# Projection products that stream their moving operand from the last column to the first

## The chip, the cores and the metric

One core of a Trainium2 chip runs the whole program. The metric is device time in microseconds (us) of one launch. The kernel before took 895.56 us in the median of three runs (894.59 to 895.74).

## The reference, cut to what matters

Two transformer-like blocks in float32 over one sequence of 256 tokens and a model width of 1024. The first block normalizes x, multiplies it by `w_in` (1024 x 8280), runs a gated delta rule over 8 heads and a sparse attention with an indexer, multiplies by `w_out`, and adds an MLP with squared ReLU (1024 x 4096 and 4096 x 1024). The second block has an input projection (1024 x 3592), retention and forgetting attention, a cross attention to 256 memory rows, and a gated MLP with hidden width 2816.

```python
proj = h @ w_in                                        # first block
x = x + merged @ w_out
x = x + jnp.square(jax.nn.relu(h2 @ w_mlp_up)) @ w_mlp_down
proj = hn @ w_in                                       # second block
h = h + (jax.nn.silu(hn @ w_gate[l]) * (hn @ w_up[l])) @ w_down[l]
```

The change touches only how the products of activations with weight matrices (the projections) are streamed through TensorE. What is computed stays the same: every output column is the same sum, in the same order over the contracted dimension.

## The kernel before, in words

**Blocks and chunks.** Every weight matrix is cut into column blocks, mostly 512 wide (`NCOL`); some are 300, 260 or 256 wide. The list `blocks` (lines 122 to 152) holds them in the order in which they are computed. A block is loaded in chunks of `CK` = 4 row tiles of 128, into a ring of four slots (`raw`, and in the same ring `w_hi` and `w_lo`). SyncE issues the loads (`load`, line 398); a load waits on `mm_done` of the chunk four before it.

**Split numbers.** A float32 operand is carried as two float32r parts. ScalarE writes `w_hi` from `raw` (line 1273), VectorE (line 1826), or in a few chunks GpSimd (line 2638), writes `w_lo` as the rest. The activations are turned by TensorE, and lie as `s_hi` and `s_lo` (or `hT_hi`, `hT_lo`, `h2_hi`, `h2_lo` for the two down projections), with 128 rows of the contracted dimension on the partitions and the 256 tokens along the free dimension. A product then takes three matmuls: high by high, high by low, low by high.

**`mm` (line 477).** It computes one block for all 256 tokens, two row tiles of the contraction at a time (a "pair", or "quarter" of a block of eight tiles). `product` (line 493) issues one matmul: the stationary operand is a 128 x 128 piece of the activations, the moving operand is a row tile of the weight chunk, `width` columns wide, and the output is bank `G[b % 2][t]`, for token tile t. All the matmuls of a block accumulate in the same two banks; consecutive ones mostly alternate between the banks. Two sets of two banks alternate between blocks, so that ScalarE and VectorE can read one set while TensorE fills the other.

**`up` (line 978).** The first MLP's up projection is computed turned: the stationary operand is a 128 x 128 piece of the weights (`w`), the moving operand is one row tile of the activations, all 256 tokens, and the output is a bank of `UP_BANKS` (`tile_product`, line 991). Three of these follow each other into the same bank.

**Between the projections** TensorE runs the small float32 matmuls and transposes of the mixers: transposes (lines 560, 607, 670, 707, 742, 1144, 1177, 1233), logits and weighted sums (lines 659, 684, 1166, 1194), the delta rule's products (lines 754 to 961). Line 758 is a float32 matmul of 512 moving columns, line 1166 one of 256. Line 855 reads its moving operand in runs of 16 columns with gaps of 16 (`blocks_of`, line 382). Each of these keeps its form under the change. All of TensorE's work is in one program order, written out by hand: quarters of projections are placed between the mixers' steps so that TensorE has work while other engines prepare the next operand.

**Who reads the banks.** ScalarE's `project` (line 1287) and VectorE's counterparts wait for `mm_done` of the whole block and then read the bank in rising order; the residual of the last block is added on VectorE (line 1851).

Of the kernel before, what the change touches and what calls it, by code (L numbers as in the profile page):

```python
# [12 lines left out]
SEQ = 256  # L13
# [91 lines left out]
def build(nc, x_in, norm_mix_g, w_in, conv_w, a_log, dt_bias, gdn_norm_g, q_norm_g, k_norm_g, w_out,  # L105
# [4 lines left out]
    with ctx:  # L110
        def sb(name, shape, dt=F32, stack=None):
            return (stack or ctx).enter_context(nc.sbuf_tensor(name, shape, dt))
# [3 lines left out]
        def sem(name):  # L116
            if name not in named:
                named[name] = ctx.enter_context(nc.semaphore(name))
            return named[name]
# [45 lines left out]
        s_hi = sb("s_hi", [P, KT, SEQ], F32R)  # L165
        s_lo = sb("s_lo", [P, KT, SEQ], F32R)
# [9 lines left out]
        G = [[ctx.enter_context(nc.psum_tensor(f"gemm{s}{t}", [P, NCOL], F32)) for t in range(NT)] for s in range(2)]  # L176
        M = [ctx.enter_context(nc.psum_tensor(f"mixbank{i}", [P, NCOL], F32)) for i in range(4)]

        UP_BANKS = [[G[0][0], G[0][1], G[1][0], G[1][1]], M]
# [178 lines left out]
        def at(base, step, i):  # L358
            return base if i is None else base + step * i

        def chunk_shape(b, c):
            return min(CK, blocks[b]["kt"] - CK * c), blocks[b]["n"]
# [11 lines left out]
        def pool_chunk(b, c):  # L374
            return (b, c) in BY_POOL
# [98 lines left out]
        def _(pe):  # L474
            act_w = (s_hi, s_lo)

            def mm(b, i=None, stat=act_w, turned=None, hidden=None, quarters=None):

                blk = blocks[b]  # L480
                pairs = range(blk["kt"] // 2) if quarters is None else quarters
                if b >= 2 and pairs[0] == 0:

                    pe.wait_ge(sem("ev0"), at(b - 1, 2, i))
                    pe.wait_ge(sem("ev1"), at(b - 1, 2, i))
                for pair in pairs:
                    c = 2 * pair // CK
                    n = blk["chunk0"] + c
                    kn, width = chunk_shape(b, c)
                    early = b in EARLY and 2 * pair == blk["kt"] - 2  # L490
                    tiles = [(kt, t) for kt in (2 * pair, 2 * pair + 1) for t in range(NT)]

                    def product(kt, t, low_x=False, low_w=False):

                        lhs = stat[low_x][:, kt, P * t:P * t + P]
                        rhs = (w_lo if low_w else w_hi)[:, n % SLOTS, kt - CK * c, 0:width]
                        return nc.tensor.matmul(G[b % 2][t][:, 0:width], lhs, rhs, start=kt == 0 and not (low_x or low_w),  # L497
                                                stop=kt == blk["kt"] - 1 and (low_x if ends_low_x else low_w))

                    def low_weights():  # L500

                        if b == 0:
                            pe.wait_ge(sem("split_lo" if pair % 2 else "first_lo"), c + 1)
                        elif 2 * pair == CK * c:
                            pe.wait_ge(sem("split_lo_pool" if pool_chunk(b, c) else "split_lo"), at(low_parts(b, c), 4, i))

                    ends_low_x = True
                    if turned is not None:
                        if b == 0:
                            pe.wait_ge(sem("split_hi" if pair % 2 else "first_hi"), c + 1)  # L510
                            if pair == 0:
                                pe.wait_ge(sem("vec_dve"), 2)
                        elif 2 * pair == CK * c:
                            pe.wait_ge(sem("split_hi"), n + 1)
                        pe.wait_ge(sem("turn_hi"), turned - KT // 2 + pair + 1)
                        for kt, t in tiles:
                            product(kt, t)
                        low_weights()
                        for kt, t in tiles:
                            product(kt, t, low_w=True)  # L520
                        pe.wait_ge(sem("turn_lo"), turned - KT // 2 + pair + 1)
                        for kt, t in tiles:
                            last = product(kt, t, low_x=True)
                    elif early:
                        low_weights()
                        if hidden is not None:

                            pe.wait_ge(sem(hidden), pair + 1)
                        for kt, t in sorted(tiles, key=lambda tile: tile[1]):
                            product(kt, t)  # L530
                            product(kt, t, low_w=True)
                            last = product(kt, t, low_x=True)
                            if t == 0 and kt == blk["kt"] - 1:
                                last.then_inc(sem("first_tile"), 1)
                    else:
                        ends_low_x = False
                        if 2 * pair == CK * c:
                            pe.wait_ge(sem("split_hi"), at(n + 1, 4, i))
                        if hidden is not None:

                            pe.wait_ge(sem(hidden), pair + 1)
                        for kt, t in tiles:
                            product(kt, t)
                        for kt, t in tiles:
                            product(kt, t, low_x=True)
                        low_weights()
                        for kt, t in tiles:
                            last = product(kt, t, low_w=True)
                    if kt == CK * c + kn - 1:
                        last.then_inc(sem("mm_done"), 1)  # L550
# [427 lines left out]
            def up(b, i=None):  # L978

                first = b == 0 and i is None
                if b < 2 and i is None:
                    pe.wait_ge(sem("ev0"), B_UP)
                    pe.wait_ge(sem("ev1"), B_UP)
                    if b == 1:
                        pe.wait_ge(sem("turn_lo"), 12)
                else:
                    pe.wait_ge(sem("ev0"), at(B_UP + b - 1, 2, i))
                    pe.wait_ge(sem("ev1"), at(B_UP + b - 1, 2, i))

                def tile_product(kt, f, low_x=False, low_w=False):
                    n = blocks[B_UP + b]["chunk0"] + kt // CK
                    w = (w_lo if low_w else w_hi)[:, n % SLOTS, kt % CK, P * f:P * f + P]
                    return nc.tensor.matmul(UP_BANKS[b % 2][f][:, 0:SEQ], w, (s_lo if low_x else s_hi)[:, kt, :],  # L994
                                            start=kt == 0 and not (low_x or low_w), stop=kt == KT - 1 and low_x)

                def tile_products(kt, f):
                    tile_product(kt, f)
                    tile_product(kt, f, low_w=True)
                    return tile_product(kt, f, low_x=True)  # L1000

                pe.wait_ge(sem("split_lo"), at(low_parts(B_UP + b, 0), 4, i))
                if first:

                    for pair in range(CK // 2):
                        tiles = [(kt, f) for kt in (2 * pair, 2 * pair + 1) for f in range(4)]
                        pe.wait_ge(sem("turn_hi"), 12 - KT // 2 + pair + 1)
                        for kt, f in tiles:
                            tile_product(kt, f)
                        for kt, f in tiles:  # L1010
                            tile_product(kt, f, low_w=True)
                        pe.wait_ge(sem("turn_lo"), 12 - KT // 2 + pair + 1)
                        for kt, f in tiles:
                            last = tile_product(kt, f, low_x=True)
                else:
                    for kt in range(CK):
                        for f in range(4):
                            last = tile_products(kt, f)
                last.then_inc(sem("mm_done"), 1)
                pe.wait_ge(sem("split_lo"), at(low_parts(B_UP + b, 1), 4, i))  # L1020
                if first:
                    pe.wait_ge(sem("turn_lo"), 12)
                for f in range(4):
                    for kt in range(CK, KT):
                        last = tile_products(kt, f)
                    if f < 3:
                        last.then_inc(sem("up_pe"), 1)
                last.then_inc(sem("mm_done"), 1)
# [1757 lines left out]
```

## Time and profile before

| What | Value |
|---|---|
| median of three runs | 895.56 us (894.59 to 895.74) |
| the profiled execution's own time | 895.47 us |
| its span, first to last instruction | 893.7 us |
| TensorE matmuls (PE) | 886.9 us busy, 99% of the span, 5035 instructions |
| TensorE weight loads (PEld) | 764.6 us, 86% |
| VectorE / ScalarE / GpSimd | 587.4 / 447.4 / 113.0 us busy |
| granted TensorE clock | 1.0 of full speed |
| HBM read | 147.59 MB, 167 GB/s over the span |

PE is busy from when a matmul starts to when its last result is written. Matmuls overlap, so the duration of one is longer than the distance from its start to the next one's start. It is that distance, and not the duration, that a stretch of matmuls is made of; it is read from the chain of waits, which gives a stretch's length and its count. PEld runs beside PE. An engine's idle time is listed with what ended it.

### The profile page before, as it was taken

What the parts mean: (1) busy time and instruction counts of PE and PEld (TensorE: products, weight loads), DVE (VectorE), ACT (ScalarE), POOL (GpSimd) and SP (SyncE); (2) the same over time, 40 slices, a digit from 0 to 9 for tenths busy, and PEclk for the clock granted to TensorE, in tenths of its full rate; (3) what the DMA queues carried; (4) which work ended last, traced back from release to release, by engine and by line L of the source; (5) the groups of instructions that cost most, each with busy time, mean ns of one, the idle gap of its engine ahead of it and who ended that gap; (6) DMA issues with size and microseconds to landing.
All of it is one profiled execution on the core that took longest, in us unless ns stands there. A gap on an engine that the chain in (4) does not pass through costs nothing.

```text
span 893.7 us, 12639 instructions
## 1 busy us (share of the span) xinstructions
PE 886.9 (99%) x5035; PEld 764.6 (86%) x5035; DVE 587.4 (66%) x856; ACT 447.4 (50%) x631; POOL 113.0 (13%) x85
## 2 busy tenths in 40 slices
PE   9999999999999999999999999999999999999998
PEld 6887887888988999988888889888888888889886
DVE  5378988996796566644456657877776565554542
ACT  6265456865455545533344436646554544444431
POOL 0431225755110000000000002100100000000200
PEclk9999999999999999999999999999999999999999
DMA  8874542435144555555577535524532565554562
GB/s 299 203 246 144 187 142 95 134 115 151 60 143 149 184 186 188 188 188 188 189 242 251 188 96 189 188 95 141 166 131 82 187 190 188 186 166 148 190 227 71
DMA packets 83554, 149.74 MB, mean 168 GB/s; under 512 B 8480, under 2 KB 16208, under 8 KB 83376
## 3 DMA queue, kind: packets, MB, share of 16 engines
q1 hardware_dynamic: 80352, 144.55, 49.8%
q10 hardware_dynamic: 2528, 3.63, 1.1%
q0 software_dynamic: 624, 0.87, 0.9%
q8 instruction: 35, 0.57, 0.2%
q14 instruction: 15, 0.12, 0.0%
HBM read 147.59 MB, written 1.44 MB: 167 GB/s over the span
## 4 chain that ended last, share of the span: by engine, by line
PE 97%; DMA 2%; ACT 0%; DVE 0%; issue 0%; SPq 0%
PE gemm L497 72%; PE mixbank L994 5%; PE gemm L994 5%; PE mixbank L560 2%; DMA raw<-in_w_in_dram 1%; PE mixbank L659 1%; PE mixbank L684 1%; PE mixbank L764 1%; PE mixbank L855 1%; PE mixbank L1166 1%; PE gemm L1194 1%; PE mixbank L670 1%; DMA x<-in_x_dram 1%; PE mixbank L1233 1%; PE mixbank L707 1%; PE mixbank L1083 0%
## 5 line engine op out<-in xcount | busy, mean ns | idle before, releaser
L1826 DVE TENSOR_TENSOR w_lo<-raw,w_hi 128x2048 fp32r<-128x2048 f32 (+3 forms) x131 | 285.4, 2189 | 185.6 <-ACT w_hi L1273 185.5
L1273 ACT ACTIVATE w_hi<-raw 128x2048 fp32r<-128x2048 f32 (+3 forms) x140 | 255.2, 1832 | 171.3 <-DMA raw<-in_w_in_dram 51.1
L497 PE MATMUL gemm<-w_hi,s_hi 128*128 128x512 f32 (+3 forms) x784 | 209.1, 387 | 0.4 <-ACT s_hi L1297 0.3
L497 PE MATMUL gemm<-w_lo,s_hi 128*128 128x512 f32 (+3 forms) x784 | 201.7, 377 | 0.1
L497 PE MATMUL gemm<-w_hi,s_lo 128*128 128x512 f32 (+3 forms) x784 | 201.7, 377 | 0.0
L497 PEld LDWEIGHTS gemm<-w_lo,s_hi 128*128 128x128 f32 x784 | 142.7, 188 | 27.6 <-DVE w_lo L1826 0.3
L497 PEld LDWEIGHTS gemm<-w_hi,s_lo 128*128 128x128 f32 x784 | 142.7, 188 | 27.5
L497 PEld LDWEIGHTS gemm<-w_hi,s_hi 128*128 128x128 f32 x784 | 139.5, 188 | 26.3 <-issue 2.5
L2644 POOL TENSOR_TENSOR sm<-sm 128x2 f32<-128x2 f32 (+5 forms) x13 | 21.5, 1660 | 455.7 <-DVE sm L1870 299.2
L2638 POOL TENSOR_TENSOR w_lo<-raw,w_hi 128x2048 fp32r<-128x2048 f32 x9 | 41.4, 4609 | 156.7 <-ACT w_hi L1273 156.7
L1290 ACT ACTIVATE mix<-gemm,sm 128x512 f32<-128x512 f32 (+2 forms) x25 | 16.3, 652 | 51.0 <-PE gemm L497 51.0
L994 PE MATMUL mixbank<-s_hi,w_hi 128*128 128x256 f32 x128 | 36.2, 283 | 0.0
L994 PE MATMUL mixbank<-s_hi,w_lo 128*128 128x256 f32 x128 | 36.2, 283 | 0.0
L994 PE MATMUL mixbank<-s_lo,w_hi 128*128 128x256 f32 x128 | 36.2, 283 | 0.0
L497 PE MATMUL gemm<-w_hi,hT_hi 128*128 128x512 f32 x128 | 34.7, 389 | 0.0
L497 PE MATMUL gemm<-w_hi,hT_lo 128*128 128x512 f32 x128 | 34.7, 389 | 0.0
L497 PE MATMUL gemm<-w_lo,hT_hi 128*128 128x512 f32 x128 | 34.7, 389 | 0.0
L994 PE MATMUL gemm<-s_hi,w_hi 128*128 128x256 f32 x128 | 34.0, 284 | 0.0
L994 PE MATMUL gemm<-s_hi,w_lo 128*128 128x256 f32 x128 | 33.9, 283 | 0.0
L994 PE MATMUL gemm<-s_lo,w_hi 128*128 128x256 f32 x128 | 33.9, 283 | 0.0
L2070 DVE SCALAR_TENSOR_TENSOR mix<-mixbank,cw,mix 128x255 f32<-128x255 f32 (+2 forms) x72 | 29.0, 471 | 1.6 <-ACT mix L1423 1.5
L497 PEld LDWEIGHTS gemm<-w_hi,hT_lo 128*128 128x128 f32 x128 | 24.0, 188 | 5.0
(353 smaller groups left out, 1162.5 us busy)
## 6 DMA issues: line engine op xcount, KB each, us to landing
raw<-in_w_in_dram SPq DMA_DIRECT2D x40, 1024.0 KB, 5.1
raw<-in_w_mlp_up_dram SPq DMA_DIRECT2D x16, 1024.0 KB, 5.6
raw<-in_w_mlp_down_dram SPq DMA_DIRECT2D x16, 1024.0 KB, 5.1
raw<-in_w_gate_dram SPq DMA_DIRECT2D x10, 1024.0 KB, 5.1
raw<-in_w_up_dram SPq DMA_DIRECT2D x10, 1024.0 KB, 5.1
raw<-in_w_down_dram SPq DMA_DIRECT2D x10, 1024.0 KB, 5.0
raw<-in_w_out_dram SPq DMA_DIRECT2D x8, 1024.0 KB, 5.2
raw<-in_w_xkv_dram SPq DMA_DIRECT2D x8, 1024.0 KB, 5.1
```

What stands on the lines that cost most here:

```text
L497: return nc.tensor.matmul(G[b % 2][t][:, 0:width], lhs, rhs, start=kt == 0 and not (low_x or low_w), stop=kt == blk["kt"] - 1 and (low_x i ...
L560: last = nc.tensor.transpose(M[q][:, (2 * kk + t) * P:(2 * kk + t + 1) * P], src(2 * q + kk, t), ident)
L659: last = nc.tensor.matmul(M[g % 2][:, j * ns:(j + 1) * ns], qq[:, P * t:P * t + P], kk[:, 0:ns], start=e == 0, stop=e == len(parts) - 1)
L670: last = nc.tensor.transpose(M[2][:, c * P:(c + 1) * P], exps[:, g % 2, c * P:(c + 1) * P], ident)
L684: last = nc.tensor.matmul(outs[k % len(outs)][:, j * width:(j + 1) * width], exps_turned[:, g % 2, (j * per + s) * P:][:, 0:P], values(h, ...
L994: return nc.tensor.matmul(UP_BANKS[b % 2][f][:, 0:SEQ], w, (s_lo if low_x else s_hi)[:, kt, :], start=kt == 0 and not (low_x or low_w), st ...
L1273: nc.scalar.activation(w_hi[:, n % SLOTS, 0:kn, 0:width], raw[:, n % SLOTS, 0:kn, 0:width], ACT.Copy)\
L1290: nc.scalar.activation(dst, G[b % 2][0][:, 0:blocks[b]["n"]], ACT.Copy, scale=scale).then_inc(sem("ev0"), 1)
L1826: V.tensor_tensor(w_lo[:, s, 0:kn, 0:width], raw[:, s, 0:kn, 0:width], w_hi[:, s, 0:kn, 0:width].bitcast(F32), ALU.subtract)\
L2070: ins = V.scalar_tensor_tensor(y, M[CONV_BANK[s]][:, SEQ * j:SEQ * j + SEQ - tap], cw[:, 3 - tap, ct:ct + 1], y, ALU.mult, ALU.add)
L2638: pool.tensor_tensor(w_lo[:, s, 0:kn, 0:width], raw[:, s, 0:kn, 0:width], w_hi[:, s, 0:kn, 0:width].bitcast(F32), ALU.subtract)\
L2644: pool.tensor_tensor(dst, src, MHALF[:, 0:n], ALU.pow).then_inc(sem("root"), 1)
```

## The change

In `mm` the output and the moving operand are both given with a step of -1 along the free dimension, starting at their last column. In `up` the same is done to the bank and to the activations. Operands, order of the instructions, waits, signals, stationary operands and the `start` and `stop` flags stay. The matmuls of the mixers and the transposes are not touched.

```diff
@@ product, line 493
                         lhs = stat[low_x][:, kt, P * t:P * t + P]
                         rhs = (w_lo if low_w else w_hi)[:, n % SLOTS, kt - CK * c, 0:width]
-                        return nc.tensor.matmul(G[b % 2][t][:, 0:width], lhs, rhs, start=kt == 0 and not (low_x or low_w),
+                        return nc.tensor.matmul(G[b % 2][t][:, 0:width][:, ::-1], lhs, rhs[:, ::-1], start=kt == 0 and not (low_x or low_w),
                                                 stop=kt == blk["kt"] - 1 and (low_x if ends_low_x else low_w))
@@ tile_product, line 991
                     w = (w_lo if low_w else w_hi)[:, n % SLOTS, kt % CK, P * f:P * f + P]
-                    return nc.tensor.matmul(UP_BANKS[b % 2][f][:, 0:SEQ], w, (s_lo if low_x else s_hi)[:, kt, :],
+                    return nc.tensor.matmul(UP_BANKS[b % 2][f][:, 0:SEQ][:, ::-1], w, (s_lo if low_x else s_hi)[:, kt, ::-1],
                                             start=kt == 0 and not (low_x or low_w), stop=kt == KT - 1 and low_x)
```

## Rows read from the trace of the kernel before

**Rows 1.** The page's busy time by engine, and TensorE's busy and clock in 40 slices.

```profile
PE 886.9 (99%) x5035; PEld 764.6 (86%) x5035; DVE 587.4 (66%) x856; ACT 447.4 (50%) x631; POOL 113.0 (13%) x85
...
PE   9999999999999999999999999999999999999998
...
PEclk9999999999999999999999999999999999999999
```

**Rows 2.** The page's shares of the chain of waits, by engine.

```profile
PE 97%; DMA 2%; ACT 0%; DVE 0%; issue 0%; SPq 0%
```

**Rows 3.** Waits of TensorE: us in total, times, longest.

```profile
PE gemm L571 <- DVE mix L1882: 1.6, 1, 1.6
PE mixbank L684 <- DVE mix L2028: 0.3, 1, 0.3
```

**Rows 4.** Groups of matmuls by line and shape: count | busy us, mean ns | idle before.

```profile
L497 PE MATMUL gemm<-w_hi,s_hi 128*128 128x512 f32 x688 | 192.7, 400 | 0.4 <-ACT s_hi L1297 0.3
...
L994 PE MATMUL mixbank<-s_hi,w_hi 128*128 128x256 f32 x128 | 36.2, 283 | 0.0
...
L497 PE MATMUL gemm<-w_hi,hT_hi 128*128 128x512 f32 x128 | 34.7, 389 | 0.0
...
L994 PE MATMUL gemm<-s_hi,w_hi 128*128 128x256 f32 x128 | 34.0, 284 | 0.0
...
L497 PE MATMUL gemm<-w_hi,h_hi 128*128 128x512 f32 x88 | 24.1, 390 | 0.0
...
L497 PE MATMUL gemm<-w_hi,s_hi 128*128 128x300 f32 x32 | 5.9, 305 | 0.0
...
L497 PE MATMUL gemm<-w_hi,s_hi 128*128 128x260 f32 x32 | 5.3, 289 | 0.0
L497 PE MATMUL gemm<-w_hi,s_hi 128*128 128x256 f32 x32 | 5.2, 285 | 0.0
```

**Rows 5.** The chain of waits in order of time (start us, us, what): projection stretches.

```profile
282.30 11.52 PE gemm L994 x96
...
374.46 87.07 PE gemm L497 x384
...
532.50 5.90 PE gemm L497 x48
```

**Rows 6.** Timeline of TensorE, 300-column products; four groups of four lie between these.

```profile
41.42 0.71 PE L497 MATMUL gemm<-w_hi,s_hi 128*128 128x300 f32 x4
...
44.15 0.70 PE L497 MATMUL gemm<-w_lo,s_hi 128*128 128x300 f32 x4
```

**Rows 7.** Timeline around 305 us: matmuls of `up` and the weight loads beside them.

```profile
305.18 0.28 PE L994 MATMUL gemm<-s_hi,w_hi 128*128 128x256 f32 x1
305.18 0.19 PEld L994 LDWEIGHTS gemm<-s_hi,w_lo 128*128 128x128 f32 x1
305.30 0.28 PE L994 MATMUL gemm<-s_hi,w_lo 128*128 128x256 f32 x1
```

**Rows 8.** The chain of waits in order of time: float32 matmuls of the mixers.

```profile
146.79 1.72 PE gemm L758 x4
...
208.83 7.09 PE mixbank L855 x64
...
658.35 1.73 PE mixbank L1166 x8
```

**Rows 9.** The same float32 matmuls as groups by line and shape.

```profile
L1166 PE MATMUL mixbank<-mix 128*128 128x256 f32 x32 | 7.4, 379 | 0.0
...
L758 PE MATMUL gemm<-mix,cst 128*128 128x512 f32 x8 | 3.8, 593 | 0.0
```

**Rows 10.** The chain's last pieces.

```profile
835.79 54.47 PE gemm L497 x240
...
890.28 0.69 DVE x L1851
```

## The prediction

> **What bounds the kernel now.** I read four views, in this order. First the page: matmuls fill 99% of the span, in all 40 slices but the last at nine tenths or more, and the granted clock is full speed throughout, the 2.4 GHz level; VectorE stands at 66% and ScalarE at 50% [rows 1]. Then the chain of waits: 97% of it is TensorE [rows 2]. Then TensorE's own waits: the longest is 1.6 us at the start, the next 0.3 us [rows 3]. So nothing that another engine or a transfer does is waited for, and the time is the sum over TensorE's instructions of the distance from one start to the next. Only a change of that distance, or a new wait, can move the end.
>
> Last, what the distances are. By shape, the products that the change touches are [rows 4]: 512 columns, three kinds each of 688, 128 and 88, which is 2712 matmuls; 256 columns, 6 x 128 of line 994 and 3 x 32 of line 497, which is 864; 300 columns and 260 columns, 96 each. Together 3768 of 5035. The durations (389 ns and 283 ns for 512 and 256 columns) are not their cost, because they overlap; the chain gives it [rows 5]: 87.07 us for 384 matmuls is 226.7 ns for 512 columns, 11.52 / 96 is 120.0 ns for 256, and 5.90 / 48 is 122.9 ns for 260. For 300 columns, 20 starts lie between 41.42 and 44.15 us [rows 6], so 136.5 ns. Between 256 and 512 columns the distance grows by 106.7 ns, 0.417 ns a column, which is one column in each cycle of the full clock. What is left over, 226.7 - 512 x 0.417 = 13.3 ns, is a fixed cost of a start. The touched work is 2712 x 0.2267 + 864 x 0.1200 + 96 x 0.1365 + 96 x 0.1229 = 614.8 + 103.7 + 13.1 + 11.8 = 743.4 us, 83% of the time. No slack lies over any of it: a nanosecond more at each of the 3768 is 3.8 us on the end.
>
> **The change, part by part.** *Instructions, waits, signals, DMAs.* None is added, removed or moved, on any queue. Cost nothing, and no cover is needed for it.
>
> *The weight loads.* The stationary operand keeps its direction. A load of 0.19 us starts with the matmul before its own and lies beside it [rows 7]. Nothing.
>
> *Who reads the bank.* Evictions wait for whole blocks, so it doesn't matter which column is written last. At the very end a residual of 0.69 us and the store follow the last product [rows 10], as before. Nothing.
>
> *Accumulation.* Two successive matmuls into one bank both begin at the same column, now the last. Each column is revisited as long after as before: in `up`, where three follow each other into one bank, after 120 ns [rows 7]. No new dependence, nothing.
>
> *Reading and writing with step -1.* This is the only term with a price that could be large, and no row of this trace has a falling pattern. I bound it from the nearest rows.
> Lower end: the fixed part of a start. Line 758 is a float32 matmul of 512 columns that takes 1.72 / 4 = 430.0 ns, and line 1166 one of 256 that takes 1.73 / 8 = 216.3 ns [rows 8]; they grow by 0.835 ns a column, half the products' rate, and leave 430.0 - 427.4 = 2.6 ns for a start. The fixed part thus can differ by 13.3 - 2.6 = 10.7 ns between two kinds of matmul here, and I bound what another pattern could save or add in it by that. 3768 x 10.7 ns = 40.3 us, down to 855.2 or up to 935.8 us.
> Upper end: the rate. These same float32 rows show the engine streaming at half the columns per cycle. If a falling pattern threw the products back to that, 512 columns would cost 430.0 - 226.7 = 203.3 ns more, 256 columns 216.3 - 120.0 = 96.3, 300 columns (216.3 + 44 x 0.835) - 136.5 = 116.5, and 260 columns 219.6 - 122.9 = 96.7. The sum is 551.3 + 83.2 + 11.2 + 9.3 = 655.0 us.
> The one matmul whose moving pattern isn't a plain run, line 855 with runs of 16 columns, takes 7.09 / 64 = 110.8 ns for 64 columns [rows 8]. By the float32 rate its columns need only 53 ns, so a penalty of up to twice would be hidden below the spacing, which the weight load sets. It excludes nothing on step.
> I take zero for this term. A falling run touches the same addresses in the same neighbourhoods as a rising one: every block here has an even width and starts on an even column, so columns 511 and 510, 509 and 508 are the same adjacent pairs as before. A memory that serves neighbouring words together serves these together, unless the hardware only joins them in rising order.
>
> The Trainium skill has a rule that speaks against the change: "Any non-contiguous AP significantly slows down matmuls" (Advanced Engine Details and Errata, Memory Cachelines), with lines of 16 bytes in SBUF and of 8 bytes in PSUM. Read as "step +1 or slow", it makes the rival below; read by lines, four falling columns still share one SBUF line and two one PSUM line, and nothing is lost. No row here decides between the readings.
>
> **The sum.** The profiled execution took 895.47 us, of which 893.7 us is the span and 1.8 us lies around it. The terms are all zero: 895.5 us. This execution lies 0.1 us under the median of the three runs, 895.56, which themselves spread over 0.13%; about 0.2%, 1.8 us, is what a measurement of this kernel can tell from no change.
>
> **The rivals.** *Half rate (the slower side).* Place: the column stream of each of the 3768 products, whether in reading SBUF or in writing the bank. Price 655.0 us: 895.5 + 655.0 = 1550.5 us. It decides as soon as either end fails to join falling neighbours, and both at once would cost the same, since the slower end sets the pace. For it: the products run at one column per cycle, which the float32 matmuls of this trace don't reach [rows 5, 8], so the products are the form with the least room, and any element-by-element fallback shows at once with TensorE at 99% [rows 1]. Against it: the pairs argument. Chance 0.21. The Trainium skill's rule quoted above, by its first reading, is this rival.
>
> *A partial loss of rate*, as where each line crossing costs a little: between 936 and 1550 us. Chance 0.05.
>
> *A dearer start.* The first columns come from the far end of a row, and the pipeline may need some nanoseconds more to begin. From 0.5 ns a start it leaves the 1.8 us band (3768 x 0.5 ns = 1.9 us); its bound is 935.8 us. A quarter of the bound, 2.7 ns, would give 905.6 us. For it: a fixed part of 13.3 ns exists and differs by kind of matmul. Against: the address of the first column is as known as before. Chance 0.12.
>
> *A cheaper start.* The same term with the other sign: down to 855.2 us. Nothing in the rows says why a falling pattern would start sooner. Chance 0.03.
>
> *The change doesn't do what it says*: both patterns fall, so the builder could turn both round again and emit the old instruction. 895.5 us, chance 0.02.
>
> **How the numbers follow.** No effect has 0.57, and with the untouched-instruction case 0.59 within 0.2%. Faster has 0.03; slower has 0.21 + 0.05 + 0.12 = 0.38. The predicted time is the likeliest case's, 895.5 us; its own range is 893.7 to 897.3 us. With the dearer start it holds only 0.71, so the range for 8 times in 10 has to reach to half rate: 893.5 to 1552 us. It is wide because the cases lie apart, not because any one is vague.
>
> **What the changed profile would show.** Right: stretches like the 384 products of the first down projection still take about 87.1 us and the 96 of `up` 11.5 us [rows 5]; durations stay at 389 and 283 ns [rows 4]; TensorE's waits stay under 2 us. Half rate: the durations rise to those of the float32 rows, 593 and 379 ns [rows 9], the down stretch to about 165 us (384 x 0.430), VectorE's share falls under 40%, and the mixers' rows are unchanged. A dearer start: the 256- and 512-column distances grow by the same nanoseconds. If only the 512-column or only the 256-column products moved, the loss would sit in one operand: the first read weights, the second mostly activations. A new wait of TensorE on another engine would prove me wrong on the parts that I cost at nothing.

## The result and the profile after

The changed kernel took 909.96 us in the median (909.79 to 910.31, four runs), against 895.49 us for the kernel before (894.59 to 895.74): ratio 1.0162, 95% interval 1.0150 to 1.0174. That is 14.5 us slower. The profiled execution's span grew from 893.7 to 908.0 us.

The page shows the same picture as before [rows 1], only longer; instruction counts are the same.

```profile
PE 901.0 (99%) x5035; PEld 763.8 (84%) x5035; DVE 588.1 (65%) x856; ACT 447.3 (49%) x631; POOL 112.6 (12%) x85
...
PEclk9999999999999999999999999999999999999999
```

TensorE's waits, the same view as [rows 3], come to 3.4 us in all against 3.0 us before. The two longest are:

```profile
PE gemm L571 <- DVE mix L1882: 1.6, 1, 1.6
PE gemm L497 <- ACT s_hi L1300: 0.4, 1, 0.4
```

The second, 0.4 us, is the only new one, so at most 0.4 of the 14.3 us of span are waiting. The chain of waits in order of time, against [rows 5] and [rows 8], shows where it went. Its columns are the start and the length in us, the engine, tile and line, and the count of instructions; first the products that the change touches:

```profile
286.08 11.36 PE gemm L994 x96
...
376.96 89.60 PE gemm L497 x384
...
539.40 5.96 PE gemm L497 x48
...
848.57 56.02 PE gemm L497 x240
```

The same chain, steps among the short ones between them:

```profile
148.69 1.72 PE gemm L758 x4
...
211.58 7.09 PE mixbank L855 x64
...
667.40 1.73 PE mixbank L1166 x8
```

A product of 512 columns now takes 89.60 / 384 = 233.3 ns from start to start, 6.6 ns more than the 226.7 ns before. A product of 256 columns takes 11.36 / 96 = 118.3 ns, 1.7 ns *less*. 260 columns take 124.2 ns instead of 122.9. The mixers' matmuls, which were not touched, take what they took. The groups by line and shape say the same in durations, 389 to 397 ns and 283 to 282 ns:

```profile
L497 PE MATMUL gemm<-w_hi,hT_hi 128*128 128x512 f32 x128 | 35.6, 397 | 0.0
...
L994 PE MATMUL mixbank<-s_hi,w_hi 128*128 128x256 f32 x128 | 36.0, 282 | 0.0
```

If all 2712 wide products paid the full 6.6 ns, that would be 17.9 us; the 768 of `up` give back 1.3 us. Summed from start to start over the whole trace, the 512-column products grew by 16.2 us, 6.0 ns each. The difference lies in the short stretches between the mixers' steps, where twelve products take 2.81 us instead of 2.75, only 5 ns each. All 864 products of 256 columns give back 1.4 us, and the 300-column products and the transposes of line 560, with the short waits among them, take 0.3 us less each. That leaves the 14.3 us of the span.

### The profile page after: what moved, and what is told of

The parts are those of the page before. It is cut to its first block, busy times and chain, and to the rows that moved or that the text cites. A ratio compares the mean times of both kernels' runs of the same rounds, so it can differ in the third digit from the quotient of the medians.

```text
span 908.0 us, 12639 instructions
## 1 busy us (share of the span) xinstructions
PE 901.0 (99%) x5035; PEld 763.8 (84%) x5035; DVE 588.1 (65%) x856; ACT 447.3 (49%) x631; POOL 112.6 (12%) x85
## 4 chain that ended last, share of the span: by engine, by line
PE 99%; ACT 0%; DVE 0%; issue 0%; ACTq 0%
PE gemm L497 74%; PE gemm L994 5%; PE mixbank L994 5%; PE mixbank L560 2%; PE mixbank L659 1%; PE mixbank L684 1%; PE mixbank L764 1%; PE mixbank L855 1%; PE mixbank L1166 1%; PE gemm L1194 1%; PE mixbank L670 1%; PE mixbank L1233 1%; PE mixbank L707 1%; PE gemm L571 0%; PE mixbank L1083 0%; PE mixbank L742 0%
## 5 line engine op out<-in xcount | busy, mean ns | idle before, releaser
L497 PE MATMUL gemm<-w_hi,s_hi 128*128 128x512 f32 (+3 forms) x784 | 213.0, 393 | 0.8 <-ACT s_hi L1300 0.4
L497 PE MATMUL gemm<-w_lo,s_hi 128*128 128x512 f32 (+3 forms) x784 | 206.3, 384 | 0.0
L497 PE MATMUL gemm<-w_hi,s_lo 128*128 128x512 f32 (+3 forms) x784 | 206.3, 384 | 0.0
```

Of the source, the lines that this page charges most:

```text
L497: return nc.tensor.matmul(G[b % 2][t][:, 0:width][:, ::-1], lhs, rhs[:, ::-1], start=kt == 0 and not (low_x or low_w), stop=kt == blk["kt" ...
```

## The experiments

Thirteen kernels ran. Seven are the real kernel with one thing changed; five leave the whole computation out and run nothing but rows of matmuls; one, x3, is a candidate for a better kernel. The order below is the order in which they ran.

**Which of the two patterns costs: e1 and e2.** Each keeps one half of the change. Both leave the columns of every product mirrored, so what comes out is not the reference; the work is the same.

```diff
 e1: nc.tensor.matmul(G[b % 2][t][:, 0:width], lhs, rhs[:, ::-1], ...)          # and likewise in up
 e2: nc.tensor.matmul(G[b % 2][t][:, 0:width][:, ::-1], lhs, rhs, ...)
```

> Only the moving operand falls; the bank is written in rising order. This leaves every projection's columns mirrored in the output of each product, so the values are not the reference's; the work and its order are unchanged. Theory R (the cost is in reading the moving operand, which shares SBUF with the weight load beside it): all of the change comes back, 512-column products at 233.3 ns and 256-column ones at about 118.3 ns from start to start, span about 908 us. Theory W (the cost is in writing the bank): the distances are those of before, 226.7 and 120.0 ns, span about 893.7 us.

> Only the bank is written in falling order; the moving operand is read in rising order. Products are mirrored in their columns, with the same amount of work. Theory R: distances of before, 226.7 and 120.0 ns, span about 893.7 us. Theory W: 233.3 and 118.3 ns, span about 908 us. If both ends have a share, the two runs' excesses over 893.7 us add up to 14.3 us.

Measured: e1 909.53 us, span 907.7; e2 895.63 us, span 893.8 (one run each). The first down projection in the chain of e1:

```profile
376.71 89.61 PE gemm L497 x384
```

The same row of e2:

```profile
374.59 87.07 PE gemm L497 x384
```

All of the cost is in reading the moving operand. Writing the bank from its last column to its first costs nothing. Theory R holds, W falls.

**Only the narrow products: e3.**

```diff
-G[b % 2][t][:, 0:width][:, ::-1], lhs, rhs[:, ::-1], ...
+(G[b % 2][t][:, 0:width] if width > 256 else G[b % 2][t][:, 0:width][:, ::-1]), lhs, (rhs if width > 256 else rhs[:, ::-1]), ...
```

> The change is kept for the 864 products of 256 columns (the up projection and the last two gate and up blocks) and undone for the wider ones. By the distances of the changed kernel it should lie 864 x 1.67 ns = 1.4 us under the kernel before, ratio 0.998, if the distance belongs to the shape and not to its surroundings; a fixed dearer start (the rival of the prediction) would give over 1.000.

Measured: 893.92 us against 895.45, ratio 0.9983 (0.9974 to 0.9992), that is 1.5 us under the kernel before. `up` is at 11.36 us for 96, and the wide products are back where they were. The first stretch of `up` in its chain:

```profile
282.11 11.36 PE gemm L994 x96
```

This beats both kernels. It also says that one dearer start for every product, the rival as the prediction put it, is wrong: falling is dearer for wide products and cheaper for narrow ones.

**Matmuls alone on the chip: m1.** The kernel has one TensorE program: for each segment, 24 float32r matmuls, alternating between two banks, with four stationary and four moving pieces in turn. A `mark` (one small float32 matmul on a line of its own, two instructions) separates the segments, so that the chain lists each segment as a row. The core of it:

```
lhs = s[:, at:at + m]                                  # m = 128 unless said
rhs = turn(w[:, k // 2 % 4, 0:n], moving)              # turn: [:, ::-1] where it falls
nc.tensor.matmul(turn(G[k % 2][0:m, 0:n], bank), lhs, rhs, start=k < 2, stop=k >= 22)
```

> No part of the reference is computed: 60 segments of 24 matmuls each, alone on the chip, alternating between two banks. Widths 128 to 512 with moving operand and bank rising or falling separately; stationary operands of 32, 64, 96 and 128 columns; a stationary operand with step 2; shifted stationary addresses; float32 and bf16. Theory R: the distance follows the moving direction alone, and because the moving stream competes with the weight load, the fixed part shrinks with the stationary columns, from 13.3 ns at 128 to some 5 ns at 32, and grows with step 2; the falling distance at 256 columns changes with the stationary operand's address (in the changed kernel it lies between 115 and 123 ns). float32 shows no difference of direction, since it streams at half the rate. Theory W: the distance follows the bank's direction alone, and neither the stationary operand's width nor its address matters. A fixed dearer start: falling minus rising is the same at every width.

The first five segments and a part of the sixth, at the start of the run, take 213 ns a matmul whatever their width (128 or 192 columns); segments of these two widths are left out. For the others I took the mean distance between starts, without the first four matmuls of a segment:

| columns | both rise | both fall | moving falls | bank falls |
|---|---|---|---|---|
| 256 | 119.7 | 118.3 | 118.4 | 119.5 |
| 320 | 146.7 | 146.7 | 146.7 | 146.5 |
| 384 | 173.9 | 177.9 | 177.9 | 173.4 |
| 448 | 202.7 | 206.7 | 206.7 | 202.7 |
| 512 | 228.3 | 233.3 | 233.4 | 228.3 |

The four segments of 512 columns in the chain (rise, fall, moving falls, bank falls):

```profile
120.25 5.54 PE gemm L89 x24
...
125.96 5.66 PE gemm L89 x24
...
131.78 5.66 PE gemm L89 x24
...
137.61 5.54 PE gemm L89 x24
```

The 228.3 ns is a mean over a run-in. In the rising segment the distances scatter between 224 and 236 ns from the second to the tenth, and from the eleventh on they are 226 or 227 ns, the kernel's value. The falling segment is at 233 or 234 ns from the second distance on. Once settled, the gap at 512 columns is thus the kernel's 6.6 ns. Falling costs nothing or less at 256 and 320 columns and more at the wider ones, so its price is neither the same for every start nor in proportion to the columns.

Nothing else runs beside them, so neither VectorE, ScalarE nor a DMA has a part in the price. It follows the moving operand's direction alone, as R says. But R's second half failed: with only 32 stationary columns a rising 512-column product takes 231.7 ns and a falling one 233.4 ns, not some 5 ns of fixed part. The two directions also cost the same in the other number formats: falling and rising take the same row in float32 and in bf16. Float32 has x48, since each matmul is two instructions of 429.2 ns at 512 columns.

```profile
259.44 20.66 PE gemm L89 x48
...
280.26 20.66 PE gemm L89 x48
...
306.66 5.18 PE gemm L89 x24
...
312.01 5.18 PE gemm L89 x24
```

In bf16 a matmul of 512 columns takes 215.8 ns, 2.5 ns over its columns; in float32r 13 to 20 ns over. So float32r products take 11 to 18 ns more each than bf16, which reads half the bytes per column. Neither bf16 nor float32, which streams half the columns per time, shows a difference of direction. The Trainium skill gives a gap of N / 2.4 + 2.5 ns for an isolated matmul (TensorE: Matmul & The Clock Gate, Back-to-back issue gap). That agrees with the bf16 rows here, 215.8 ns at 512 columns, and is too low for float32r. The falling order adds to the excess of float32r.

**Placement: m2.** The stationary operand is moved by 0 to 60 columns and by 128.

> No part of the reference is computed: segments of 24 float32r matmuls of 512 and of 256 columns, rising and falling, with the stationary operand moved by 0 to 60 columns (4 bytes each) and by 128 against the moving operand. [...] Rival F (a falling read has a price of its own, whatever else reads): falling lies 6.7 ns over rising at 512 columns at every shift, and 1.7 ns under it at 256 columns.

Against Rival F stood that the distance is set by where the two operands lie against each other, and spreads more when the moving one falls. At 512 columns rising, the distance lies between 226.7 ns (shifts 4 and 60) and 233.9 ns (shift 24), and at 12 of the 20 shifts at 232 or above; shift 0, where the kernel before is, gives 228.3. Falling, it is 233.3 ns at 18 of 20 shifts, among them 0, and 236.7 ns at the other two (36 and 60). At 256 columns rising it lies between 115.8 and 120.0 ns, falling between 117.7 and 120.1. So placement matters, which Rival F denied, but in these segments a falling read hardly sees it, where it was expected to spread more. Falling is not a price on top; it is a floor of 233.3 ns in place of one of 226.7 ns, and the kernel before happens to sit on the rising floor.

**Placement in the real kernel: x1 and x2.** Both put a tile of 28 unused columns ahead of `s_hi` and shorten the tile `phase` to 84.

```diff
+        sb("shift", [P, 28])
         s_hi = sb("s_hi", [P, KT, SEQ], F32R)
...
-        sb("phase", [P, 112])
+        sb("phase", [P, 84])
```

> The kernel before, with rising patterns, and 28 unused columns (112 bytes) in front of s_hi, so that s_hi and s_lo lie 28 columns later against the weights; the tile 'phase' is 28 columns shorter, so that the mixer regions, hT_* and h2_* stay where they were. Theory P (direction has no price of its own; a falling read only loses the favourable alignment of the two operands that the kernel before has): its 2064 products of 512 columns with s_* go from 226.7 to 233.3 ns, as alone on the chip at this shift, the 648 with hT_* and h2_* stay at 226.7 ns, and the time grows by 2064 x 6.7 ns = 13.8 us to about 909 us, the same as with falling patterns. Rival F (falling reads cost something by themselves, and placement is a side effect of the short test): nothing changes, 895.5 us.

> The changed kernel with the same 28 columns in front of s_hi. Theory P: its 512-column products are already at the unfavourable distance and stay at 233.3 ns, so about 910 us, within 1 us of the changed kernel, and rising and falling are level once placement is the same. Rival F: the price of direction and that of placement add up, 910 us or more, and 14 us above the rising kernel with the same placement.

```profile
376.57 89.59 PE gemm L498 x384
```

That is 233.3 ns, and m2 gave 233.0 ns for a shift of 8. The long stretches with `s_*` take 22.30 / 96 = 232.3 ns, and m2 gave 232.4 for a shift of 32. A rising kernel that is merely placed elsewhere loses 12.6 of the changed kernel's 14.5 us. Rival F (14 us between the directions at the same placement) is out, since the two lie 4.9 us apart. Of Theory P the first half holds, that a placement can cost as much as the turn does. Its second half missed: the directions are not level at one placement, and x2 lies 3 us over the changed kernel instead of within 1. Summed from start to start over the two traces, the difference lies in the 512-column products with `s_*` (4.2 us, 2 ns each) and in `up` (1.0 us).

**Each operand's own address: m3.**

> No part of the reference is computed: segments of 24 float32r matmuls. The moving operand alone is shifted (by 4, 16, 28, 60 columns), then both operands by the same amount; one stationary piece, one moving piece or one bank throughout; finer and larger shifts of the stationary operand; widths of 300 and 260 columns. Theory P with a relative phase: shifting both operands alike gives the distances of shift 0 (about 227 to 228 ns at 512 columns rising), shifting the moving one alone by k gives what shifting the stationary one by -k gave. If each operand's own address counts, shifting both does not bring the distance back. Repetition of the pattern: shifts of 64, 68, 92 and 124 columns give what 0, 4, 28 and 60 gave. One bank throughout changes nothing. If what counts is the meeting of one stationary piece with the next, one fixed stationary piece changes the distance.

At 512 columns rising, shifting both by 4 gives 233.4 ns, by 28 or 60 gives 230.0, by 16 gives 228.3 as at shift 0. So it is not the relative address alone; by these shifts each operand's own place within 64 bytes counts as well. One stationary piece (227.3 ns), one moving piece or one bank (228.3) change nothing but the run-in; all three settle at 226.7 ns. Falling stays at 233.3 to 233.5 ns in all eleven segments. The shift of 64 settles at 226.7 ns as shift 0 does, but 68 gave 233.5 where 4 had given 226.7 in m2, and 124 gave 228.3 where 60 had given 226.7, against the expected repetition. m4, whose tiles are those of m3, brings it back: there 4, 28 and 60 give 233.3, 233.3 and 228.3 ns, and m3 has 233.5, 233.2 and 228.3 for 68, 92 and 124.

**A grid, and a version that should have been better: m4 and x3.** x3 puts `s_hi` and `s_lo` in one tile and starts them 4 columns in.

```diff
-        s_hi = sb("s_hi", [P, KT, SEQ], F32R)
-        s_lo = sb("s_lo", [P, KT, SEQ], F32R)
+        s_both = sb("s", [P, 2 * KT * SEQ + 8], F32R)
+        s_hi, s_lo = (s_both[:, 4 + KT * SEQ * k:4 + KT * SEQ * (k + 1)].rearrange("p (k s) -> p k s", k=KT) for k in range(2))
...
-        sb("phase", [P, 112])
+        sb("phase", [P, 104])
```

> No part of the reference is computed: a grid of placements, moving operand shifted by 0, 4, 8, 12 columns, stationary by 0 to 60 in steps of 4, 16 float32r matmuls each; 512 columns rising, 256 rising, 512 falling. Theory P2 (each operand's address within 256 bytes sets the distance; falling reads never reach the favourable value): rising at 512 columns lies between 226.7 and some 237 ns with the low value at few placements, falling stays at 233.3 ns or above at all 64; none reaches the 216 ns of bf16. Rival F2 (falling has favourable placements of its own, which the kernel doesn't use): some falling placement lies under 230 ns.

> The kernel before, rising, with s_hi and s_lo 4 columns (16 bytes) later in SBUF and everything else in its place. From the segments alone on the chip: 512-column products stay at 226.7 ns (stationary operand shifted by 4), the up projection, where s_* is the moving operand, goes from 120.0 to 116.9 ns, so 768 x 3.1 = 2.4 us come off, about 893.1 us, ratio 0.9973. If placement counts only in the short test, 895.5 us.

In m4, 6 of the 64 rising placements lie at 226.7 to 226.8 ns, none lower, and the highest at 236.7. With only 16 matmuls a segment the run-in weighs more: by their last three distances, 9 placements, shift 0 among them, have settled at 226.7 ns. All 64 falling ones lie between 233.25 and 236.7 ns, 55 of them at 233.3. F2 is out: none of these placements rescues the falling read. But a stationary shift of 4 columns, at 226.7 ns in m2, stood at 233.3 ns here; at 14 of the 16 shifts that both have, all but 4 and 60, they agree to about 1 ns. The two runs differ in what ran before and in the tiles that lie in front of the stationary one, so they don't say which of the two matters. And x3 missed: 902.17 us, ratio 1.0072 (1.0058 to 1.0085), not 893.1. Its trace shows both values:

```profile
376.60 87.09 PE gemm L497 x384
...
745.82 22.39 PE gemm L497 x96
...
769.09 21.78 PE gemm L497 x96
```

The `hT_*` products, left in place, take 226.8 ns. Those with `s_*` take 233.2 ns in the second row, as mostly, and 226.9 in the third, though both rows are two blocks of the same form that go once through the same four slots. So at some placements a stream of products can run at either value within one execution. That it depends on what ran before is the likely reading and was not tested. `up` came down to 11.39 / 96 = 118.6 ns, and not to 116.9.

**The order inside the read: m5.** The bank always rises; the moving operand is cut into groups, and either the groups fall and the columns in them rise (outer -1, inner 1) or the other way round.

```
rhs = w[:, frm:frm + n].rearrange("p (a b) -> p a b", b=group)[:, ::outer, ::inner]
```

> No part of the reference is computed: 24 float32r matmuls per segment, the bank always rising. The moving operand is read in groups of 2 to 128 columns, groups falling with columns rising inside, and the other way round; a stationary operand that is one column read 128 times; a moving operand that is one column read over and over. Theory L (what counts is the order in which groups of addresses of both reads are visited): falling groups of 64 or 128 columns with rising insides behave like rising (226 to 228 ns at 512 columns), small falling groups (2 and 4) behave like falling, 233.3 ns, whatever the order inside; with one stationary column there is nothing left to meet, and rising and falling come down towards the 216 ns of bf16 alike. Rival I (the order inside a small group is what costs, as when neighbouring words are joined only in rising order): rising groups with falling insides cost as much as a plain fall at every size, and falling groups with rising insides cost nothing from groups of 4 on; one stationary column changes neither.

Distances at 512 columns (ns):

| group | groups fall, columns in them rise | groups rise, columns in them fall |
|---|---|---|
| 2 | 233.4 | 228.3 |
| 4 | 233.4 | 228.3 |
| 8 | 233.4 | 233.3 |
| 16 | 233.3 | 266.7 |
| 64 | 227.2 | 233.4 |
| 128 | 228.3 | 233.3 |

The chain's rows for groups of 4 (both orders), then 16 (rising groups, falling insides), 64 (both orders), and last the moving operand that is one column read 512 times:

```profile
55.55 5.66 PE gemm L82 x24
...
61.37 5.54 PE gemm L82 x24
...
84.56 6.45 PE gemm L82 x24
...
91.17 5.52 PE gemm L82 x24
...
96.86 5.66 PE gemm L82 x24
...
125.76 5.27 PE gemm L82 x24
```

Inside 4 columns, which are 16 bytes, the order doesn't matter. Between groups of 64 columns (256 bytes) it doesn't either; groups of 32 were not tried. What costs is the order of the 16-byte pieces within a stretch of 256 bytes: a plain fall does, and so do groups of 8 or 16 columns in either arrangement. The dearest are the rising groups of 16 columns with falling insides, at 266.7 ns for 512 columns and 133.3 for 256: twice as much for twice the columns, so here it is a price per column, a quarter over the 0.417 ns.

When the moving read stays on one column, the distance drops to 217.3 ns, near bf16's. With one stationary column read 128 times, falling stays at 233.3 and rising at 228.7 ns: so falling is dearer whatever addresses the stationary read visits, against my theory since e1 that the meeting of the two reads makes it so. The loss needs a moving read that walks through SBUF. It isn't the moving read's alone when it rises, since m2 moved only the stationary operand and went from 226.7 to 233.9 ns. Rival I is out, and of Theory L the part on groups held while the part on the stationary operand failed.

**In the kernel itself: y1 and y2.** The groups of 64 in all products of 512 and 256 columns, on the moving operand and on the bank alike; products of 300 and 260 columns rise.

```diff
+        def order(ap):
+            if ap.shape[-1] % 64:
+                return ap
+            return ap.rearrange("p (a b) -> p a b", b=64)[:, ::-1, ::1]      # y1; y2 has [:, ::1, ::-1]
...
-nc.tensor.matmul(G[b % 2][t][:, 0:width], lhs, rhs, ...)
+nc.tensor.matmul(order(G[b % 2][t][:, 0:width]), lhs, order(rhs), ...)
```

> All 512- and 256-column products read the moving operand, and write the bank, in groups of 64 columns: the groups from the last to the first, the columns inside a group rising (products of 300 and 260 columns are left rising). Theory O (only the order of neighbouring 16-byte pieces inside 64 columns counts): 512 columns stay at 226.7 ns (227.2 alone on the chip) and 256 at 120.0, about 895.5 us, though the last column group is read first. Rival D (the overall direction counts, the start at the far end of the row): 910 us as with the plain fall.

> The reverse: groups of 64 columns from the first to the last, the columns inside a group falling; 300 and 260 columns left rising. Theory O: 512 columns at 233.3 ns and 256 at 118.3, so 2712 x 6.7 - 864 x 1.7 = 16.6 us more, about 912 us at most, and near the changed kernel's 910. Rival D: 895.5 us, as everything starts at the first group and runs forward.

Measured: y1 895.78 us, ratio 0.9999 (0.9990 to 1.0009); y2 909.76 us, ratio 1.0158 (1.0141 to 1.0175). The first down projection in the chain of y1:

```profile
376.66 87.07 PE gemm L502 x384
```

The same row of y2:

```profile
377.02 89.61 PE gemm L502 x384
```

y1 begins each product in its last 64 columns and goes backwards, and costs nothing. y2 begins at the first and goes forwards, and costs what the change costs. `up` follows too: 11.52 us for 96 in y1, as before, and 11.36 in y2, as changed. Theory O holds in the kernel, and Rival D is out.

## Why the prediction was wrong, point by point

- **What bounds the kernel**: right. TensorE is busy throughout before and after, the one new wait is 0.4 us, and the sum of the distances came out one for one at the end. One reading is off: the float32 rows count instructions, and m1 shows two of them to a matmul. The 430.0 ns is half a float32 matmul of 512 columns. The rate within an instruction, which the bounds use, stays.
- **Instructions, weight loads, evictions, accumulation**: right to cost at nothing. e2 shows it for the bank's order, and m3's segments show 228.3 ns rising and 233.4 falling whether or not the accumulation alternates between banks.
- **Reading and writing with step -1**: this is the term that failed. I took zero, on the ground that a falling run touches the same neighbouring words. That ground is true as far as it goes: up to groups of 4 columns the order is free (m5). It isn't the whole of the read. The order in which the 16-byte pieces follow each other within 256 bytes has a price of its own, at the kernel's placement 6.6 ns at 512 columns, and -1.7 ns at 256. The term measured +14.3 us of span, and lay inside the bounds that I had drawn from the float32 rows for a start, -40.3 to +40.3 us. That it did is luck in part: those bounds were drawn for the fixed part of a start, and what moved is not the same at every width.
- **The rival "a dearer start"** came nearest in time, with 905.6 us at a quarter of its bound and 935.8 us at the whole. Its size fits, its mechanism does not: it said the same nanoseconds at every width. I gave 0.12 to it. I had noticed a fixed part of 13.3 ns that float32 lacks, and treated it as a cost of starting. Most of it goes when the moving read stays on one column (m5's 217.3 ns), so it depends on how SBUF is read, and a new pattern of reading could be expected to move it. Nothing in the trace before told the two readings apart.
- **Half rate**: no sign of it. **A partial loss of rate** was priced from 936 us up and so missed the time, but it comes nearest in kind. Falling minus rising grows with the width in m1, from -1.4 ns at 256 columns over 0 at 320 and 4.0 at 384 to 5.0 at 512 (6.6 once settled), and the order of 16-byte pieces is what counts in m5, though not by a cost for each crossing, since the number of crossings is the same both ways. I gave it 0.05.
- **The Trainium skill's rule**, "Any non-contiguous AP significantly slows down matmuls" (Advanced Engine Details and Errata, Memory Cachelines), stands there under PSUM, and the prediction took it for both ends. It is not borne out for a step of -1: on the PSUM side the price is none (e2), on the SBUF side 3% at 512 columns (e1). The 16-byte lines that the page gives for SBUF do show, as the size up to which order is free in m5.
- **The change doesn't do what it says**: out; e1 and e2 differ by 14 us.
- **The range**, 893.5 to 1552 us, held the time; the forecast of no change and the 0.59 on it did not. The bounds were wide enough, and the choice of the middle was not sound: with rows that bound a price at 40 us on either side, zero was a guess.
- **The sign that I named** ("if only the 512-column or only the 256-column products moved, the loss would sit in one operand") misled: they moved in opposite directions, and m1 shows the width itself to be the reason, in one and the same operand.

Open: why the pieces' order matters, why the gap between directions turns round between 256 and 384 columns, what lets the same placement run at two values, and why x1 and x2 lie 4.9 us apart where m2 has them level to 1 ns. The runs show these and don't explain them. Whether a weight load is needed for the loss at all was not tried, since a float32r matmul always brings its own.

## What to carry to other kernels

Where TensorE is the bound, measure a read pattern's price as the distance between starts and per width; here a change that only turned a pattern round cost 1.6%, and the same turn on the 256-column products alone gained 0.17%. For float32r products, count 226.7 to 233.3 ns for 512 columns at the full clock, and check that value again after any change of SBUF layout, even a spare tile: one that moved `s_*` by 128 bytes and `hT_*` and `h2_*` by 32 cost 12.6 us here. A value from a short test is a candidate; it is confirmed only in the kernel. Leave out the run-in of a short test as well, which here lasted some ten matmuls and made 228.3 ns of 226.7.

## What the runs showed of the hardware that was not expected

- A float32r matmul of 512 columns costs 11 to 18 ns more than bf16's 215.8 ns, alone on the chip, and 217.3 ns when its moving operand is one column. Falling order in PSUM is free.
- The order of columns is free within 16 bytes and the order of stretches is free from 256 bytes on. At the sizes tried in between, 32 and 64 bytes, it isn't: rising groups of 16 columns with falling insides take 266.7 ns, far above both a plain rise (228.3, settled 226.7) and a plain fall (233.3).
- Alone on the chip, falling reads are nearly blind to placement, at 233.3 to 236.7 ns in all 64 cells of m4, while rising ones range from 226.7 to 236.7 ns. In the kernel the falling version still lost 3 us more by the placement of x2.
- One placement can run at some 227 or at 233 ns, both in one execution of x3 (21.78 and 22.39 us for 96 products).
